# First block's second attention: values stationary, exponentials transposed in waves of 1 to 4 heads, gates multiplied into the exponentials on POOL

## The reference

```python
s = jnp.einsum('tghd,cgd->tghc', qt, k_cmp).astype(jnp.float32) * scale
p_cmp = masked_softmax(s, (cmp_last[None, :] <= t[:, None])[:, None, None, :])
o_cmp = jnp.einsum('tghc,cgd->tghd', p_cmp.astype(v_cmp.dtype), v_cmp)
...
p = masked_softmax(s, (kpos <= t[:, None, None])[:, :, None, :])
o_slc = jnp.einsum('tghk,tgkd->tghd', p.astype(vsel.dtype), vsel)
...
p = masked_softmax(s, mw[:, None, None, :])
o_win = jnp.einsum('tghk,kgd->tghd', p.astype(vw.dtype), vw)
o = gt[:, 0][..., None] * o_cmp + gt[:, 1][..., None] * o_slc + gt[:, 2][..., None] * o_win
```

## Time and profile before

| what | value |
|---|---|
| median of three runs | 3292.12 us |
| lowest, highest | 3290.89, 3294.03 us |
| the profiled execution | 3289.18 us |
| its span, first to last instruction | 3287.4 us |
| mean granted TensorE clock | 0.957 |
| busy share PE, DVE, ACT, POOL | 94%, 49%, 35%, 4% |

### The profile page before, as it was taken

One profiled execution on the slowest core, in us unless ns is written; L12 is line 12 of the kernel. 1 busy time (PEld: TensorE's weight loads), 2 busy tenths in 40 slices (PEclk: granted clock), 3 DMA queues, 4 the chain that ended last, 5 costly groups with the idle time before them and its releaser, 6 DMA issues.

```text
span 3287.4 us, 40325 instructions
## 1 busy us (share of the span) xinstructions
PE 3081.9 (94%) x16164; PEld 2615.9 (80%) x16164; DVE 1626.7 (49%) x2834; ACT 1143.0 (35%) x1927; POOL 141.3 (4%) x122
## 2 busy tenths in 40 slices
PE   7899999898999999999799889999999989999998
PEld 5678887686998788878577887888888779878887
DVE  6756666645556667662244754222222455443333
ACT  3532223424453322231244653211112345432222
POOL 2010001000001000010000101000000100010001
PEclk9999999968899999999899999999999989999999
DMA  4234444231002344432100001211111110022221
GB/s 156 74 112 160 160 159 136 85 109 65 1 1 71 117 159 162 159 116 68 39 1 12 23 25 52 71 64 64 59 64 59 54 48 1 20 80 99 92 101 65
DMA packets 74985, 260.13 MB, mean 79 GB/s; under 512 B 8112, under 2 KB 10672, under 8 KB 74672
## 3 DMA queue, kind: packets, MB, share of 16 engines
q1 hardware_dynamic: 74800, 257.57, 23.3%
HBM read 255.44 MB, written 2.10 MB: 78 GB/s over the span
## 4 chain that ended last, share of the span: by engine, by line
PE 82%; DVE 7%; ACT 6%; issue 3%; DMA 2%; DVEq 0%; SPq 0%; ACTq 0%
PE PS L484 79%; PE PS L1210 3%; DVE WL L417 1%; ACT WH L411 1%; DVE SM L2084 1%; ACT Q L1139 0%; PE PS L1244 0%; DMA RAW<-in_kv_v 0%; ACT TMP L1217 0%; DMA RAW<-in_f_in 0%; ACT PB L1201 0%; ACT TMP L1201 0%; DVE XR L817 0%; DMA RAW<-in_a_in 0%; DVE Q L1256 0%
## 5 line engine op out<-in xcount | busy, mean ns | idle before, releaser
L484 PE MATMUL PS<-UH,WH 128*128 128x512 f32 x2296 | 872.4, 380 | 69.7 <-DVE UL L609 19.4
L484 PE MATMUL PS<-UL,WH 128*128 128x512 f32 x2296 | 860.2, 375 | 0.0
L484 PE MATMUL PS<-UH,WL 128*128 128x512 f32 x2296 | 856.2, 373 | 0.0
L411 ACT ACTIVATE WH<-RAW 128x1024 fp32r<-128x1024 f32 (+1 forms) x367 | 379.7, 1037 | 908.2 <-PE PS L484 591.9
L417 DVE TENSOR_TENSOR WL<-RAW,WH 128x1024 fp32r<-128x1024 f32 (+1 forms) x367 | 446.7, 1220 | 374.4 <-ACT WH L411 364.4
L484 PEld LDWEIGHTS PS<-UH,WH 128*128 128x128 f32 x2296 | 440.6, 192 | 163.1 <-DVE WL L417 30.1
L484 PEld LDWEIGHTS PS<-UL,WH 128*128 128x128 f32 x2296 | 440.5, 192 | 79.0 <-issue 5.6
L484 PEld LDWEIGHTS PS<-UH,WL 128*128 128x128 f32 x2296 | 438.9, 191 | 77.6
L484 PE MATMUL PS<-HH,WH 128*128 128x512 f32 x1008 | 368.6, 366 | 2.6 <-DVE HL L1954 2.6
L484 PE MATMUL PS<-HL,WH 128*128 128x512 f32 x1008 | 368.9, 366 | 0.0
L484 PE MATMUL PS<-HH,WL 128*128 128x512 f32 x1008 | 367.0, 364 | 0.0
(11 more groups left out here) (301 smaller groups left out, 4039.3 us busy)
## 6 DMA issues: line engine op xcount, KB each, us to landing
RAW<-in_mod_w SPq DMA_DIRECT2D x96, 512.0 KB, 3.3
RAW<-in_f_in SPq DMA_DIRECT2D x88, 512.0 KB, 3.3
RAW<-in_g_in SPq DMA_DIRECT2D x88, 512.0 KB, 3.2
RAW<-in_f_out SPq DMA_DIRECT2D x32, 448.0 KB, 3.9
RAW<-in_g_out SPq DMA_DIRECT2D x32, 448.0 KB, 3.1
RAW<-in_a_in SPq DMA_DIRECT2D x16, 512.0 KB, 3.6
RAW<-in_f_out SPq DMA_DIRECT2D x16, 512.0 KB, 4.2
RAW<-in_g_out SPq DMA_DIRECT2D x16, 512.0 KB, 3.2
```

The lines of the kernel that those rows point to most:

```text
L411: act.e.activation(hi, raw, ACT.Copy).then_inc(wh.step(n, i), 1)
L484: return pe.e.matmul(out, l, r, start=start, stop=stop)
```

## The change

- nsa_waves takes the place of nsa_units: 48 waves. A wave is a group's rows of up to 1024 exponential columns: for q = 0 four heads with both branches, for q = 1 four heads of one branch, for q of 2 and 3 two heads of one branch. So 1 compressed wave and 4, 8, 16, 16 waves for the four query blocks.
- Outputs: the values are stationary (VV, high half in columns 0 to 63 and low half in 64 to 127 of one 128x128 tile), the transposed exponentials move, as high half PTH and low half PTL, all heads of a tile in one matmul (256 or 512 columns). They add up over all waves of a group in one PSUM place; the compressed branch joins at the group's last wave (VC, PCH, PCL).
- So that the sum over waves and branches needs no factor behind it, POOL multiplies the exponentials in place by reciprocal x gate before PE transposes them.
- The transposes of a wave come three steps behind its scores, the outputs four. ACT copies all transposed columns (high half), DVE subtracts for the low half; the next transposes wait for both.
- At a group's end ACT copies the lower 64 partitions of the output, DVE adds the upper ones (high-half and low-half values), ACT and POOL write high and low half to Q2, already transposed. The flips fall away; b_out waits for POOL's last one and reads Q2 in another order (NX).
- kv and compression: VV and VC are written as high and low halves (two DVE subtractions of 128x1024 more; for VC one DVE addition, five ACT copies and one DVE subtraction in place of VBD's memset and 16 additions).
- The last 2048 columns of the constants are no longer loaded near a_in but after ctxT, since PCH, PCL and BOT lie in their space; even_vector waits for them.

The diff, cut to its core:

```diff
+    VV = at("VV", V0 + 32 * KB, [128, 4, 8, 128], F32R)
+    VC = at("VC", T0 + 13 * KB, [128, 128], F32R)
...
+    PTH = [at("PTH0", T0, [128, 1024], F32R), at("PTH1", T0 + 8 * KB, [128, 1024], F32R)]
+    PTL = [at("PTL0", T0 + 4 * KB, [128, 1024], F32R), at("PTL1", U0 + 44 * KB, [128, 1024], F32R)]
...
             if j == after("mod_w", 95):
                 sp.wait_ge(mod.after(95, 2))
                 sp.e.dma_start(CB, ctxT).then_inc(s_ctx, 16)
+                sp.wait_ge(fin.after("nsa", 3, 3, 1))
+                sp.e.dma_start(CON[:, NC2:CONST_N], consts[:, NC2:CONST_N]).then_inc(s_con3, 16)
...
+            dve.e.tensor_tensor(VV[:, k, :, 64:128], psum.at["values", i].rearrange("p (a j n) -> p a j n", a=2, j=8),
+                                VV[:, k, :, 0:64].bitcast(F32), ALU.subtract).then_inc(dve_c.step("vv", i), 1)
...
+                for g in range(4):
+                    act.wait_ge(dve_c.after("v"), dve_c.after("vc zero"))
+                    act.e.activation(v[32 * g:32 * g + 31, :], x[0:31, g, :], ACT.Copy).then_inc(act_c.step("v", g), 1)
+                act.wait_ge(act_c.after("v", 3))
+                act.e.activation(VC[:, 0:64], v, ACT.Copy).then_inc(act_c.step("vc"), 1)
...
-                for g in range(4):
-                    for h in range(4):
-                        dve.e.tensor_tensor(VBD[32 * h:32 * h + 31, g, 64 * h:64 * h + 64], o[0:31, 64 * g:64 * g + 64],
-                                            vec("cmp_b2v", 0, 64)[0:31, :], ALU.add).then_inc(dve_c.step("v", g, h), 1)
...
     def nsa_tensor(pe):
+            n = s - 3
+            if 0 <= n < len(NW):
+                q, g, rows, L, tiles, _, _ = NW[n]
+                o = psum.enter("across", "across", "nsa", n)
+                pe.wait_ge(scaled.after("nsa", n), *psum.clear("across", "nsa", n))
...
+            n = s - 4
...
+                pe.wait_ge(copy.after("nsa", n), dve_c.after("vv", 1))
...
+                for br, k, heads in tiles:
+                    N, a = 128 * len(heads), 128 * (heads[0] - 4 * g)
+                    v = VV[:, k, 4 * br + g, :]
+                    mm(pe, o[:, a:a + N], v, hi[:, c:c + N], first and br == 0 and k == 0, False)
+                    last = mm(pe, o[:, a:a + N], v, lo[:, c:c + N], False, False)
+                    c += N
+                if final:
+                    r = slice(32 * g, 32 * g + 32)
+                    pe.wait_ge(copy.after("nsa", CMP[q]), dve_c.after("vc"))
+                    mm(pe, o[:, 0:512], VC[r, :], PCH[r, :], False, False)
+                    last = mm(pe, o[:, 0:512], VC[r, :], PCL[r, :], False, True)
...
     def nsa_scalar(act):
+        for s in range(len(NW) + 7):
             n = s - 1
...
+                    for i, (_, _, c, p) in enumerate(row_places(n)):
+                        e = act.e.activation(p_of(n)[:, p:p + L], o[:, c:c + L], ACT.Exp, bias=st[:, i:i + 1], accum_out=st[:, 8 + i:9 + i])
...
+            n = s - 3
...
+                act.wait_ge(across.after("nsa", n))
...
+                    act.e.activation(PTH[PLACE[n] % 2][:, 0:N], o[:, 0:N], ACT.Copy).then_inc(evac.step("nsa", n), 1)
+                psum.leave(("across", "nsa", n), evac)
+            n = s - 5
+            if 0 <= n < len(NW) and NW[n].last:
...
+                act.e.activation(BOT[LO, :], psum.at["out", q, g][HI, :], ACT.Copy).then_inc(act_o.step("nsa", q, g, "bottom"), 1)
+            n = s - 6
...
+                act.e.activation(Q2[:, q, 4 * g:4 * g + 2, :], SUM.rearrange("p (t n) -> p t n", t=2), ACT.Copy).then_inc(act_o.step("nsa", q, g, "hi"), 1)
...
     def nsa_vector(dve):
+        for s in range(len(NW) + 6):
+            n = s - 4
+            if 0 <= n < len(NW):
...
+                dve.wait_ge(evac.after("nsa", n))
+                hi, lo = (PCH, PCL) if NW[n].g is None else (PTH[PLACE[n] % 2], PTL[PLACE[n] % 2])
+                dve.e.tensor_tensor(lo[:, 0:N], o[:, 0:N], hi[:, 0:N].bitcast(F32), ALU.subtract).then_inc(copy.step("nsa", n), 1)
+                psum.leave(("across", "nsa", n), copy)
+            if s < len(NW):
...
+                    dve.e.tensor_reduce(stat_cols(s)[:, 0:c], o.rearrange("p (b n) -> p b n", b=c)[:, :, 0:L], AX.X, ALU.max,
+                                        negate=True).then_inc(most.step("nsa", s), 1)
             n = s - 1
...
+                    dve.e.reciprocal(r, r).then_inc(recip.step("nsa", n), 1)
+            n = s - 5
+            if 0 <= n < len(NW) and NW[n].last:
...
+                dve.wait_ge(act_o.after("nsa", q, g, "bottom"), *([pool_o.after("nsa", *before_group(q, g))] if (q, g) > (0, 0) else [dve_q.after("gates")]))
...
+                for e, r in enumerate((LO, HI)):
+                    dve.e.tensor_tensor(SUM[r, :].rearrange("p (t n) -> p t n", t=2), by_head(psum.at["out", q, g][LO, :])[:, e, :, :],
+                                        by_head(BOT[LO, :])[:, e, :, :], ALU.add).then_inc(fin.step("nsa", q, g, e), 1)
...
+    def nsa_gpsimd(pool):
...
+                    pool.wait_ge(recip.after("nsa", n))
+                    pool.e.tensor_tensor(rv, rv, gv, ALU.mult).then_inc(gates_in.step(n), 1)
+                    pool.wait_ge(gates_in.after(n), expo.after("nsa", n))
+                    p = p_of(n)[:, 0:c * L].rearrange("p (h n) -> p h n", h=c)
+                    pool.e.tensor_tensor(p, p, r.unsqueeze(2).to_broadcast([128, c, L]), ALU.mult).then_inc(scaled.step("nsa", n), 1)
...
-        out_tensor(pe, "b_out", [p for m0 in (0, 4) for p in (act_o.after(("nsa", 3), m0), dve_o.after(("nsa", 3), m0))], "f1")
+        out_tensor(pe, "b_out", [pool_o.after("nsa", 3, 3)], NX, "f1")
```

More of the change, by code:

```diff
@@ L3 @@
 from concourse import mybir
+from collections import namedtuple
 from contextlib import ExitStack
@@ new lines, in nsa_waves, with earlier @@
+                for i, rows in enumerate(sets):
+                    tiles = [(br, k, [hd for hd, b in rows if b == br]) for br in sorted({b for _, b in rows}) for k in range(q + 1)]
+                    waves.append(Wave(q, g, rows, L, tiles, i == 0, i == len(sets) - 1))
+        return waves
+    NW = nsa_waves()
+    REAL = [n for n, w in enumerate(NW) if w.g is not None]
+    PLACE = {n: i for i, n in enumerate(REAL)}
+    CMP = {w.q: n for n, w in enumerate(NW) if w.g is None}
+    def earlier(n, back):
+        i = PLACE[n] - back
+        return REAL[i] if i >= 0 else None
@@ L1462, in out_tensor @@
+    def out_tensor(pe, name, done, OX, norm):
         pe.wait_ge(*done)
```

315 lines of the change are left out of this document (155 added, 160 removed).

## The result

| kernel | median us | range | ratio to before, 95% interval |
|---|---|---|---|
| before | 3291.51 | 3289.46 to 3294.03 | |
| changed | 3316.14 | 3305.71 to 3317.88 | 1.0068, 1.0045 to 1.0090 |
| forecast | 3279.4 | 3255 to 3306 | |

The profiled execution took 3305.71 us (span 3303.6), the lowest of the changed kernel's; the forecast for it was 3276.5, so the trace has 29 us of the miss, and the median lies 10 above that execution where I had allowed 3.

A forecast was written before the change was run, and what follows sets the result against it. The one-place PSUM ring (3.5 us a turn) was to replace TensorE (3.0) as bound. Terms from 810 sum to 207 us: b_out 10.2 us earlier, plus 2.5 from part 4, gives 3276.5 profiled, 3279.4 median; range 3255 to 3306.

The forecast's parts named there:

- TensorE's own wave: Block 3's scores, transposes and outputs on TensorE: 3.0 us a wave against 3.77, with 256-column matmuls at 0.12 us.
- The ring: Transposes, ACT copy and DVE subtraction take turns in one PSUM place: 3.5 us a turn, 2.8 with 768 columns.
- rival (b): Coupling of three in-order queues costs 0.3 us more a turn, 13 us over 44 turns: 3292; chance 0.18.
- POOL: free: POOL's multiply between exp and transposes takes 2.6 us, 2.9 a wave with gate and hops, under the 3.5 turn.
- The group's own gap: At a group's last wave, bottom copy and two DVE additions delay the next subtraction: 1.3 us a group.
- The overrun: The extra pair of 512-column matmuls exceeds TensorE's slack by 0.1 to 0.3 us, 2.2 us over 12 groups.
- The tail: Last copy, subtraction, outputs, bottom, sums and the high and low halves before b_out: 7.0 us.
- Groups 12 x 1.3 = 15.6: Waits at group ends added to the ring in the sum: 12 groups at 1.3 us, 15.6 us.
- Low clock after these (some 7 us each, as 881 to 891 shows): After the compressed waves of blocks 1 to 3, waves take 6.0 us instead of 3.5: 3 x 2.9 = 8.7 us.
- rival (d): Half-speed clock stays as TensorE idles 15% of each turn; half the waves at 6.0 us, 55 more: 3334; chance 0.05.
- A third set across the clock's return near 822: Block 0's start: third of four score sets before the first transposes, at the clock's return; 18.0 us from 810 with transposes.
- Part 4: Beside the stage, 16 small VBD additions become one addition and five ACT copies: 2.5 us gained, bounds 0 and 4.

The follow-up runs named there:

- late sum: Changed kernel with DVE adding a group's output halves one step later, behind the low half of the wave after next: 3281.54 us, ratio 0.9971 to before.
- buffers: Two SUM tiles and two PCH tiles, added to the kernel with halves: 3260.78 us, ratio 0.9899 to before.
- kernel with halves: The late sum with the across PSUM place filled and emptied in two halves: 3265.63 us, ratio 0.9915 to before.
- start fill: Start wide plus 8 and 4 matmuls of 512 columns in two gaps of block 0: 3306.80 us, ratio 1.0039 to before.
- repeated trace: Changed kernel run once more with nothing edited: 3312.45 us, ratio 1.0076 to before.
- start wide: Changed kernel with 36 extra 512-column matmuls while TensorE waits for the queries' low halves: 3310.22 us, ratio 1.0053 to before.
- compressed wide: The late sum with one 512-column matmul behind every second head of the compressed scores in blocks 1 to 3: 3289.47 us, ratio 0.9985 to before.

## Why the prediction was wrong

**What held.** TensorE's own wave: 0.12 us a 256-column matmul, and 2.94 us a wave once the ring was out of the way. The ring: 3.53 and 2.83 us. Its hops did not grow when three queues run in lockstep, so rival (b) is out as stated. POOL: free, at 1.89 us for 1024 columns; my 2.6 came from other forms. By half of the 4.5 us that the Trainium skill (GPSIMD Engine Reference, Elementwise) gives for 2048 columns the estimate is 2.25, nearer than those rows but still above the measured one. DVE's subtraction of 1024 columns, bounded by the maximum's 1.21, took 1.225. The group's own gap: 1.5 for 1.3. The overrun: 0.28 for 0.1 to 0.3. The tail, behind the last transposes: 8.0 in the changed kernel and 7.1 in the late sum, for 7.0.

**The miss by segments.** The stage took 235.4 us for 206.8: 4.4 more at the start, 12.6 in block 1, 8.1 in block 2, 2.9 in block 3, 0.9 in the tail, 0.3 less in block 0. Of these 28.6 us, 12.0 are group ends (27.6 for the 15.6 of "Groups 12 x 1.3 = 15.6"), which the late sum takes away. The other 16.6 it keeps: 4.4 at the start, 1.1 in block 0, 6.2 in block 1, 3.8 in block 2, 1.1 in block 3, each against the forecast less its group ends. The start is treated below. The cause of the rest stays open; what the runs show of it is that in block 1 the buffers took 6.0 us off, in the kernel with halves.

**The step that failed: "Low clock after these (some 7 us each, as 881 to 891 shows)".** I charged low clock to the three compressed waves only, and dismissed rival (d) because TensorE 90% busy had full clock elsewhere. The mean busy share did not show it: the idle time comes in one piece of 1.9 us or more at a group's end. What the forecast called a gap of 1.3 us a group was a gap of 1.5 and, behind many of them, some 3.4 us at half clock (933 to 936, 1015 to 1018) in which TensorE, not the ring, was late: the turn behind 1014.50 took 4.52 us, that behind 998.60, at full clock, 3.53. Filling the gaps of blocks 1 to 3 was worth 9 us with their waits untouched.

**A missed wait.** In the sum's queue on DVE I named the bottom copy and the additions, not that SUM is a single tile: the addition waits for POOL's low half of the group before, which waits for ACT's high half. With a group for every one or two waves in blocks 0 and 1 this was 11.9 us of waiting and, by two tiles, about 10 us on the path, the low clock that goes with it included. So the 9 and the 10 overlap. The wait stands in blocks 0 and 1 alone, and block 1 has the largest part of the miss.

**Groups of block 0.** I charged 12 groups and counted block 0's four as ACT's work. The block itself came out at 18.9 for 19.2, which is luck: the sum had it at full clock, it ran at half clock for its first 11.3 us, and nearly all at full clock (start fill) it took 15.3.

**The start, 4.4 us.** "A third set across the clock's return near 822" carried a time of the old kernel over to new work. There the return stood 2.7 us behind the first of the VBD matmuls that the change removes; the new order has only narrow ones up to 839.56.

**Part 4.** Nothing of its 2.5 us came back. Block 0 starts 1.7 us earlier than in the trace before, but the compression's last matmuls, ahead of the VBD work, stand 1.8 us earlier already (720.68 for 722.51), and from these to block 0's first score it is 87.6 us for 87.5; the repeated trace starts block 0 at 811.41. ACT's squares, behind the values' copies, a table load of 1.28 us and two weight roundings in its queue, still hold TensorE, 2.41 us for 2.46:

```profile
737.38 0.70 PE L493 MATMUL PS<-TMP,CON 128*128 128x512 f32 x1 [2.41 <-ACT TMP L914]
```

The prediction gave this reason for a loss, with a bound of 0, but took 2.5.

**The range.** It ended at 3306 since the clock stood in it as one rival of 0.05 with one price for whole blocks. The mechanism was named; its smaller form, a little after many groups, was not priced, nor that a missed wait which makes gaps adds to it.

What stays open: how much of the remaining 22 us of the late sum is the gap of 1.5 x 16 and how much the coupling with POOL. The two runs overlap and were not made together. Open too is why one group's end is followed by low clock and the next is not. The changed kernel's executions, which spread over 12 us, go with this: the lowest has a mean granted clock of 0.951, the others 0.948 and 0.949, and the turn behind the group's end near 1000 is 4.46 us in one trace, 3.53 in the other.

## What to carry to other kernels

When a change turns TensorE from the bound into one that waits, list the longest single idle piece of each period, not the mean share, and price a fall of the clock behind it in the range. In an in-order queue put work that nobody needs soon (here a sum over finished outputs) behind the step that frees a ring, and look for tiles with one copy in every chain that crosses three engines. Where transposes, copy and subtraction take turns in one PSUM place, splitting it in two comes first: it was worth 16 us here.

## What the runs showed of the hardware

- The granted clock fell from 1.00 to 0.50 behind idle pieces of 1.57 us (start wide, 812) and 1.91 us (changed, 930), and mostly not where such pieces were filled with matmuls of 256 to 512 columns. It did not fall behind every one: of 13 idle pieces of 1.6 us or more in the changed kernel's trace behind 842, eight had it at 0.50 by 2 us after their end, five had not (2.88 us at 976 and 1.91 at 997 among them).
- Unbroken work on 128- and 32-column matmuls went on for 21 to 32 us at 0.50, and 5.2 us of 128-column ones ran at 1.00 where the clock was full when they began. In twelve traces the clock came back 1.0 to 7.3 us behind the first 256- or 512-column matmul of the low stretch at the start; with eight 512-column ones among 32 narrow ones (compressed wide) only after 13 us.
- It fell from 1.00 to 0.50 during unbroken work on 32-column matmuls (884, 942); with two 512-column ones behind every two of them it stayed at 1.00 for 198 us.
- POOL's two-input multiply with one factor broadcast along the row takes 1.89 us for 128x1024, 1.47 for 128x768 and 1.05 for 128x512; other two-input forms of 512 columns take 1.71 in this kernel.
